# Sums of squares of a residual stage: six chunks added on VectorE and summed on TensorE behind the stage's last product

## The chip, the cores and the metric

The kernel runs on one core of one Trainium2 chip. The metric is device time in microseconds (us) of one execution. TensorE does the matrix products, VectorE and ScalarE the work on their inputs and results, GpSimd only a few transfers, and SyncE's queue loads the weights.

## The reference, cut to what matters

Two transformer blocks are computed for 256 tokens of 1024 values, in float32. Five times a branch is added to the residual x, and each time an RMS norm follows, whose divisor is a sum of squares over the 1024 values of a token:

```python
def rms_norm(x, gain):
    xf = x.astype(jnp.float32)
    y = xf * lax.rsqrt(jnp.mean(xf * xf, axis=-1, keepdims=True) + RMS_EPS)
    return (y * gain.astype(jnp.float32)).astype(x.dtype)
...
        x = x + gate_m * (merged @ w_out[l])          # "x1"
        h = rms_norm(x, norm_ffn[l]) * (1.0 + scale_f) + shift_f
        u = causal_dwconv(h @ w_up[l], ffn_conv_w[l], ffn_conv_b[l])
        u_gate, u_val = jnp.split(u, 2, axis=-1)
        x = x + gate_f * ((jax.nn.silu(u_gate) * u_val) @ w_down[l])      # "x2"
...
        x = x + g1_l * y_l                            # "x3" (attention), "x5" (Fourier mix)
        h2_l = (rms_norm_2(x, norm2_g[i]) * (1.0 + sc2_l) + sh2_l).reshape(B * L, D)
...
        x = x + g2_l * f[:B * L].reshape(B, L, D)     # "x4" (feed-forward of the second block)
```

The last feed-forward is a mixture of eight experts. It takes the second half of the time, and nothing of the change lies in it.

## The kernel before

**How x lies.** X is kept transposed: 1024 values of a token lie over 8 chunks of 128 partitions, 256 tokens along the free axis. A sum over a token's values is therefore a sum over the partitions and over the chunks; TensorE makes it with a 128x128 matrix of ones (`one`) as stationary operand, all chunks accumulated in one PSUM bank ("stat").

**Products.** A weight slab (up to 2048 columns, 1 MB) comes in by SyncE's queue, ScalarE rounds it to `whi` (`act_hi`, L1267), VectorE makes the rest `wlo` (`dve_lo`, L1846), and TensorE does three products per weight tile (`three`, L632 to L634). There are NP = 3 pairs of `whi` and `wlo`: ScalarE rounds slab g + 3 once TensorE is done with slab g. `gemm` makes one output of 2 chunks (256 outputs) for all tokens.

**A residual stage.** Each of x1 to x5 ends with four such outputs, c = 0 to 3. For each of them VectorE adds the gated result to two chunks of X (`dve_residual`, L2123), ScalarE squares them into one of three buffers `sqb` (`act_residual`, L1280; 128x512), and TensorE sums the squares (`pe_stats`, L720 and L723: one product of 256 tokens for each half of the buffer). The squares of chunks 2c - 2 and 2c - 1 are summed behind output c; so the sums of chunks 0 and 1, and of 2 and 3, lie between products, that of chunks 4 and 5 directly behind the last product. (In x3 outputs 0 and 1 are made together, and both inner sums lie between outputs 2 and 3.) The last output has its two halves in two banks, so that chunk 6 can be added, squared and summed while chunk 7 is still in work; `pe_stats(.., 6, True)` sums these. Then ScalarE makes the inverse root (`act_stat`, L1294 and L1297), VectorE and ScalarE make the next stage's input (L1912, L1309, L1919), and TensorE goes on. It is kept in work in between by `spare` (L668), products whose results nobody reads, in a fixed number.

**Modulation.** The gates, scales and shifts come from vectors made on VectorE (`dve_mslabs`, L1870 and L1873, into `macc`) that TensorE sums (`pe_mods`, L709). A list says after which product each is due. x1, x3 and x4 have four of them between the last product and the sum of chunks 6 and 7; x2 has some behind its first outputs and none at its end; x5 has none.

**Order.** Each engine runs its instructions in the order written out by hand in `pe_*`, `act_*` and `dve_*`; semaphores tie them. On VectorE the c = 3 residual of x1, x3 and x5 follows the `dve_lo` of c = 2; that of x2 and x4 follows the `dve_lo` of the slab before the last.

Of the kernel before, what the change touches and what calls it, by code (L numbers as in the profile page):

```python
# [15 lines left out]
S = 256  # L16
# [183 lines left out]
def build(nc, a, out):  # L200
# [5 lines left out]
    with ctx:  # L206
# [506 lines left out]
        def pe_stats(ring, name, c, halves=False):  # L713
# [9 lines left out]
            pe.matmul(o, one[:, :], sq[:, S:512], start=False, stop=(c == 6)).then_inc(sq_read.mark(name, c), 1)  # L723
            N.note(("sq_free", name, c), sq_read.now())

        Z_G, Z_S, Z_T = (0, 1, 2), (3, 4), (5, 6, 7)

        def pe_start():
# [145 lines left out]
        def pe_branches():  # L874
            for c in range(4):
                us = [take(BR_G, "br", c, g) for g in range(4 if c == 3 else 3)]
                for s_ in range(2):
                    h, l, nk = yield from slab(st, ("br", c))
                    for part in range(2):
                        g = (0, 1, 1, 2)[2 * s_ + part]  # L880
                        apart = g == 2 and c == 3
                        for m in range(2):
                            o = us[2 + m].t[:, 0:S] if apart else us[g].t[:, m * S:(m + 1) * S]
                            for k in range(4 * part, 4 * part + 4):
                                kk = 8 * s_ + k
                                if c == 0 and m == 0:
                                    pe.wait_ge(*(yield from xlo_done.of("o", kk)))
                                first, last = ((0, 3), (4, 11), (12, 15))[g]
                                cols = slice(m * 128, (m + 1) * 128)
                                t = three(o, (h[:, k, cols], l[:, k, cols]), (OH[:, kk, :], OL[:, kk, :]),  # L890
                                          kk == first and (m == 0 or apart), kk == last)
                            if apart and m == 0:
                                t.then_inc(us[2].fill(), 1)
                        if part == 0:
                            t.then_inc(us[g].fill(), 1)
                    t.then_inc(st.slab_done.mark(st.pg - 1), 1)
                    yield from pe_mods(BR_T, 29 + 2 * c + s_)
                us[-1].told = st.slab_done.now()
            for c in range(4):
                yield from gemm(BR_G, ("out", c), ("out", c), 1, HH, HL, (lambda kk: xlo_done.of("m", kk)) if c == 0 else None, 7, c == 3)  # L900
                if c:
                    yield from pe_stats(BR_L, "x1", 2 * c - 2)
            yield from pe_mods((0, 1, 2, 6), 40.5)
            yield from pe_stats(BR_L, "x1", 6, True)

        F_G, F_T, F_L = (0, 1, 2, 3), (4, 5), (6, 7)

        def pe_ffn():
            for t in range(22):
                if t == 0:  # L910
                    yield from gemm2(F_G, (("up", 0), ("up", 1)), (("ug", 0), ("uv", 0)), HH2, HL2, lambda k: xlo_done.of("h1", k), wait=12)
                elif t > 1:
                    yield from gemm(F_G, ("up", t), (("ug", "uv")[t % 2], t // 2), 1, HH2, HL2, None, 7)
                if t in (2, 3, 6, 7):
                    tb, c4 = (t - 2) // 4, t % 2
                    u = take(F_T, "cT", tb, c4)
                    pe.wait_ge(*(yield from N.of("cn", tb)))
                    for j in range(4):
                        tt = pe.transpose(u.t[:, j * 128:(j + 1) * 128], cn[:, 0, (4 * c4 + j) * 128:(4 * c4 + j + 1) * 128], ident)
                    tt.then_inc(u.fill(), 1)  # L920
                if 10 <= t < 14:
                    yield from pe_stats(F_L, "ctx", 2 * (t - 10))
                yield from pe_mods(F_T, 41 + t)
            for c in range(4):
                yield from gemm(F_G, ("dn", c), ("dn", c), 3, FH, FL, (lambda kk: xlo_done.of("f", kk)) if c == 0 else None, 21, c == 3)
                yield from pe_mods(F_T, 65 + 3 * c)
                if c:
                    yield from pe_stats(F_L, "x2", 2 * c - 2)
            yield from pe_stats(F_L, "x2", 6, True)

        A_G, A_T = (0, 1, 2), (3, 4, 5, 6, 7)
# [44 lines left out]
        def pe_attention():  # L976
# [53 lines left out]
                             {1: lambda: side(20), 3: lambda: side(21), 4: lambda: side(22)})  # L1030
            for c in (2, 3):
                yield from gemm(A_G, ("wo", c), ("wo", c), 1, HHc, HLc, None, 7, c == 3)
                if c == 2:
                    yield from pe_stats(A_T, "x3", 0)
                    yield from pe_stats(A_T, "x3", 2)
            yield from pe_stats(A_T, "x3", 4)
            yield from pe_mods(A_T, 90.5)
            yield from pe_stats(A_T, "x3", 6, True)

        def pe_ff2():  # L1040
            yield from gemm2(F_G, (("f", 0), ("f", 1)), (("f1", 0), ("f3", 0)), HH4, HL4, lambda k: xlo_done.of("h3", k), wait=12)
            for t in range(2, 28):
                yield from gemm(F_G, ("f", t), (("f1", "f3")[t % 2], t // 2), 1, HH4, HL4, None, 7)
                yield from pe_mods(F_T, 91 + t)
            for c in range(4):
                yield from gemm(F_G, ("f2", c), ("f2", c), 4, FH4, FL4, (lambda kk: xlo_done.of("f2", kk)) if c == 0 else None, 27, c == 3)
                if c:
                    yield from pe_stats(F_L, "x4", 2 * c - 2)
            yield from pe_mods((4, 5, 7, 1), 134.5)
            yield from pe_stats(F_L, "x4", 6, True)  # L1050

        X_G, X_L = (0, 1, 2, 3, 4, 5), (6, 7)

        def pe_fourier():
            pe.wait_ge(*(yield from N.of("fcs")))
            for g in range(8):
                u = take(X_G, "fn1", g)
                if g == 0:
                    spare(u.t[:, 0:128], 9)
                pe.wait_ge(*(yield from act_step.of("fx", g)))  # L1060
                for tb in range(2):
                    t = pe.matmul(u.t[:, tb * 256:tb * 256 + 256], FX[:, g, tb * 128:tb * 128 + 128], fcs[:, 0:256], start=True, stop=True)
                t.then_inc(u.fill(), 1)
            for g in range(0, 8, 2):
                u = take(X_G, "fn2", g)
                for m in range(2):
                    pe.wait_ge(*(yield from N.of("FN", g + m)))
                    for s_ in range(4):
                        tb, part = s_ // 2, s_ % 2
                        t = pe.matmul(u.t[:, m * S:(m + 1) * S], FN[:, tb, g + m, part * 128:part * 128 + 128],  # L1070
                                      fcs[:, 256 + tb * 512 + part * 256:512 + tb * 512 + part * 256], start=(s_ == 0), stop=(s_ == 3))
                t.then_inc(u.fill(), 1)
            for c in range(4):
                yield from gemm(X_G, ("fn", c), ("fn", c), 1, HH5, HL5, (lambda kk: N.of("h4", kk)) if c == 0 else None, 7, c == 3)
                if c:
                    yield from pe_stats(X_L, "x5", 2 * c - 2)
            yield from pe_stats(X_L, "x5", 6, True)

        M_G, M_T = (0, 1, 2), (3, 4, 5)
# [1032 lines left out]
        def dve_residual(name, key, c, gate, d, g0):  # L2112
# [4 lines left out]
            for m in range(2):  # L2117
# [8 lines left out]
                else:  # L2126
                    t.then_inc(u.sem, 1)
                    N.note(("xh", name, m) if c == 3 else ("x", name, c), u.drained())

        def dve_branches():  # L2130
            for c in range(4):
                G_ = (GT1, GT2)[c // 2]
# [33 lines left out]
                yield from dve_mslabs(st.gi[31 + 2 * c + NP])  # L2166
            yield from dve_coeff("h1", 8, "norm_ffn", 0, 8)
            for c in range(4):
                yield from dve_residual("x1", "out", c, modT[0][:, 16:24], 0, 4)
                if c < 3:  # L2170
                    yield from dve_lo(st, 37 + c + NP)
# [11 lines left out]
        def dve_ffn():  # L2183
# [28 lines left out]
            for c in range(4):  # L2212
# [9 lines left out]
                if c == 3:  # L2222
                    yield from ctx
                    yield from dve_coeff("h2", 24, "n10", 1, 2)
                yield from dve_residual("x2", "dn", c, modT[0][:, 40:48], 0, 10)
            yield from dve_modulate("h2", X, HH2, HL2, 24, 1, 0, sqb)
            yield from dve_lo(st, 74 + NP)
# [53 lines left out]
        def dve_attention():  # L2281
# [29 lines left out]
            yield from dve_mods(86)  # L2311
            yield from dve_coeff("h3", 32, "n20", 1, 8)
            for c in range(4):
                yield from dve_residual("x3", "wo", c, modT[1][:, 16:24], 1, 4)
                if c < 3:
                    yield from dve_lo(st, 87 + c + NP)
# [5 lines left out]
        def dve_ff2():  # L2322
# [14 lines left out]
            for c in range(4):  # L2337
# [4 lines left out]
                        yield from dve_mslabs(st.gi[g + NP + 1])  # L2342
                if c == 3:
                    yield from dve_coeff("h4", 40, "n11", 3, 2)
                yield from dve_residual("x4", "f2", c, modT[1][:, 40:48], 1, 10)

        def dve_norm_full(name, dst, col):
# [9 lines left out]
        def dve_fourier():  # L2357
# [18 lines left out]
            dve.wait_ge(*(yield from dve_step.of("xb", 7)))  # L2376
            yield from dve_coeff("h5", 48, "n21", 3, 8)
            for c in range(4):
                yield from dve_residual("x5", "fn", c, modT[3][:, 16:24], 3, 4)
                if c < 3:  # L2380
                    yield from dve_lo(st, g + NP)
                g += 1
# [352 lines left out]
```

## Time and profile before

| | us |
|---|---|
| median of 3 runs | 2139.26 |
| lowest, highest | 2139.07, 2550.09 |
| the profiled execution | 2141.42 |
| its span | 2140.1 |

### The profile page before, as it was taken

What the parts mean: (1) busy time and instruction counts of PE and PEld (TensorE: products, weight loads), DVE (VectorE), ACT (ScalarE), POOL (GpSimd) and SP (SyncE); (2) the same over time, 40 slices, a digit from 0 to 9 for tenths busy, and PEclk for the clock granted to TensorE, in tenths of its full rate; (3) what the DMA queues carried; (4) which work ended last, traced back from release to release, by engine and by line L of the source; (5) the groups of instructions that cost most, each with busy time, mean ns of one, the idle gap of its engine ahead of it and who ended that gap; (6) DMA issues with size and microseconds to landing.
All of it is one profiled execution on the core that took longest, in us unless ns stands there. A gap on an engine that the chain in (4) does not pass through costs nothing.

```text
span 2140.1 us, 30800 instructions
## 1 busy us (share of the span) xinstructions
PE 2071.0 (97%) x12749; PEld 1844.1 (86%) x12749; DVE 1709.2 (80%) x1846; ACT 1260.1 (59%) x1270; POOL 39.4 (2%) x77
## 2 busy tenths in 40 slices
PE   4999999899999999999999999999999999999997
PEld 4887899899898999999997888888888888888886
DVE  6777787799768776777547989898888988888886
ACT  3457643545443454344346777777777777777775
POOL 3000000000000000000000000000000000000000
PEclk8999999989999999999999999999999999999999
DMA  9853476467764346888727999999999999999993
GB/s 311 269 172 113 148 249 198 157 212 245 237 197 165 135 158 199 292 293 269 228 69 274 366 359 357 356 360 363 356 362 350 362 360 358 358 359 361 361 372 146
DMA packets 332802, 580.73 MB, mean 271 GB/s; under 512 B 10357, under 2 KB 150155, under 8 KB 332656
## 3 DMA queue, kind: packets, MB, share of 16 engines
q1 hardware_dynamic: 329152, 572.57, 76.7%
q0 software_dynamic: 3008, 5.78, 1.2%
q8 instruction: 104, 1.70, 0.3%
q10 hardware_dynamic: 496, 0.33, 0.1%
q14 instruction: 42, 0.34, 0.0%
HBM read 577.56 MB, written 1.07 MB: 270 GB/s over the span
## 4 chain that ended last, share of the span: by engine, by line
PE 84%; DVE 9%; ACT 3%; issue 2%; DMA 0%; SPq 0%; DVEq 0%; ACTq 0%
PE bk L638 14%; PE bk L640 14%; PE bk L639 14%; PE bk L632 9%; PE bk L634 9%; PE bk L633 9%; DVE macc L1873 3%; DVE wlo L1846 2%; PE bk L709 1%; ACT whi L1267 1%; PE bk L1159 1%; PE bk L694 1%; DVE uc L2192 1%; PE bk L695 1%; PE bk L696 1%
## 5 line engine op out<-in xcount | busy, mean ns | idle before, releaser
L1846 DVE TENSOR_TENSOR wlo<-raw,whi 128x2048 fp32r<-128x2048 f32 x475 | 1080.6, 2277 | 264.7 <-ACT whi L1267 263.9
L1267 ACT CAST whi<-raw 128x2048 fp32r<-128x2048 f32 x475 | 902.5, 1901 | 390.2 <-PE bk L640 258.8
L632 PE MATMUL bk<-HH,whi 128*128 128x256 f32 x1480 | 430.4, 291 | 6.7 <-DVE HL L1919 6.1
L633 PE MATMUL bk<-HL,whi 128*128 128x256 f32 x1480 | 421.0, 284 | 0.0
L634 PE MATMUL bk<-HH,wlo 128*128 128x256 f32 x1480 | 420.8, 284 | 0.0
L638 PE MATMUL bk<-whi,xh 128*128 128x512 f32 x896 | 354.6, 396 | 0.0
L640 PE MATMUL bk<-wlo,xh 128*128 128x512 f32 x896 | 349.5, 390 | 0.0
L639 PE MATMUL bk<-whi,xl 128*128 128x512 f32 x896 | 348.8, 389 | 0.0
L632 PEld LDWEIGHTS bk<-HH,whi 128*128 128x128 f32 x1480 | 286.7, 194 | 11.3 <-issue 8.5
L633 PEld LDWEIGHTS bk<-HL,whi 128*128 128x128 f32 x1480 | 286.8, 194 | 1.7 <-issue 1.0
L634 PEld LDWEIGHTS bk<-HH,wlo 128*128 128x128 f32 x1480 | 286.3, 193 | 0.0
L1873 DVE SCALAR_TENSOR_TENSOR macc<-raw,csil,macc 128x512 f32<-128x512 f32 x280 | 209.9, 751 | 9.3 <-DMA raw<-in_w_mod 0.5
L640 PEld LDWEIGHTS bk<-wlo,xh 128*128 128x128 f32 x896 | 168.1, 188 | 36.0
L638 PEld LDWEIGHTS bk<-whi,xh 128*128 128x128 f32 x896 | 168.3, 188 | 34.3 <-DVE wlo L1846 1.4
L639 PEld LDWEIGHTS bk<-whi,xl 128*128 128x128 f32 x896 | 168.5, 188 | 33.3
L638 PE MATMUL bk<-whi,tth 128*128 128x512 f32 x448 | 177.5, 396 | 1.7 <-DVE ttl L2490 1.7
L640 PE MATMUL bk<-wlo,tth 128*128 128x512 f32 x448 | 177.7, 397 | 0.0
L639 PE MATMUL bk<-whi,ttl 128*128 128x512 f32 x448 | 177.5, 396 | 0.0
L632 PE MATMUL bk<-FH,whi 128*128 128x256 f32 x400 | 114.6, 286 | 0.0
L633 PE MATMUL bk<-FL,whi 128*128 128x256 f32 x400 | 113.3, 283 | 0.0
L634 PE MATMUL bk<-FH,wlo 128*128 128x256 f32 x400 | 113.2, 283 | 0.0
L638 PEld LDWEIGHTS bk<-whi,tth 128*128 128x128 f32 x448 | 84.3, 188 | 22.1 <-DVE ttl L2490 1.9
(369 smaller groups left out, 2583.0 us busy)
## 6 DMA issues: line engine op xcount, KB each, us to landing
raw<-in_moe_w SPq DMA_DIRECT2D x336, 1024.0 KB, 6.1
raw<-in_ada_w SPq DMA_DIRECT2D x48, 1024.0 KB, 5.3
raw<-in_ff_w SPq DMA_DIRECT2D x40, 1024.0 KB, 5.3
raw<-in_w_in SPq DMA_DIRECT2D x29, 1024.0 KB, 5.4
raw<-in_w_mod SPq DMA_DIRECT2D x24, 1024.0 KB, 5.6
raw<-in_w_up SPq DMA_DIRECT2D x22, 1024.0 KB, 5.1
raw<-in_attn_w_qkv SPq DMA_DIRECT2D x12, 1024.0 KB, 5.1
raw<-in_w_branch SPq DMA_DIRECT2D x8, 1024.0 KB, 5.3
```

Source lines behind the costliest of these rows:

```text
L632: pe.matmul(o, sh, mh, start=start, stop=False, skip_group_check=True)
L633: pe.matmul(o, sh, ml, start=False, stop=False, skip_group_check=True)
L634: return pe.matmul(o, sl, mh, start=False, stop=stop, skip_group_check=True)
L638: pe.matmul(o, sh, mh, start=start, stop=False, skip_group_check=True)
L639: pe.matmul(o, sl, mh, start=False, stop=False, skip_group_check=True)
L640: return pe.matmul(o, sh, ml, start=False, stop=stop, skip_group_check=True)
L694: pe.matmul(o, xh[:, k, c], h[:, k, :], start=(k == 0), stop=False)
L695: pe.matmul(o, xl[:, k, c], h[:, k, :], start=False, stop=False)
L696: t = pe.matmul(o, xh[:, k, c], l[:, k, :], start=False, stop=(k == 7))
L1267: act.copy(whi[k][:, :n], raw[q.slot[i]][:, :n]).then_inc(q.hi_done.mark(g), 1)
L1846: dve.tensor_tensor(wlo[k][:, :n], raw[q.slot[i]][:, :n], whi[k][:, :n].bitcast(F), ALU.subtract).then_inc(q.taken.mark(i), 1)
L1873: t = dve.scalar_tensor_tensor(out=acc[:, :], in0=v[:, j, :], scalar=sc, in1=acc[:, :], op0=ALU.mult, op1=ALU.add)
```

## The change

The sums of chunks 0 to 5 are no longer made one by one. `dve_squares` adds the three buffers of squares on VectorE, in two additions of 128x512, ahead of the residual of c = 3. `pe_stats_sum` sums the result over the partitions with one pair of products; it stands behind the last product and, where there are four modulation sums (x1, x3, x4), behind these. The sum of chunks 6 and 7 follows as before. The two `pe_stats` between the products are gone in all five stages.

```diff
+        def pe_stats_sum(ring, name):
+
+            u = take(ring, "stat", name)
+            pe.wait_ge(*(yield from dve_step.of("squares", name)))
+            sq = sqb[N.at["sq", name, 4]]
+            pe.matmul(u.t[:, 0:S], one[:, :], sq[:, 0:S], start=True, stop=False)
+            pe.matmul(u.t[:, 0:S], one[:, :], sq[:, S:512], start=False, stop=False).then_inc(sq_read.mark(name, 4), 1)
+            N.note(("sq_free", name, 4), sq_read.now())
...
             for c in range(4):
                 yield from gemm(BR_G, ("out", c), ("out", c), 1, HH, HL, (lambda kk: xlo_done.of("m", kk)) if c == 0 else None, 7, c == 3)
-                if c:
-                    yield from pe_stats(BR_L, "x1", 2 * c - 2)
             yield from pe_mods((0, 1, 2, 6), 40.5)
+            yield from pe_stats_sum(BR_L, "x1")
             yield from pe_stats(BR_L, "x1", 6, True)
...
                 yield from pe_mods(F_T, 65 + 3 * c)
-                if c:
-                    yield from pe_stats(F_L, "x2", 2 * c - 2)
+            yield from pe_stats_sum(F_L, "x2")
             yield from pe_stats(F_L, "x2", 6, True)
...
                 yield from gemm(A_G, ("wo", c), ("wo", c), 1, HHc, HLc, None, 7, c == 3)
-                if c == 2:
-                    yield from pe_stats(A_T, "x3", 0)
-                    yield from pe_stats(A_T, "x3", 2)
-            yield from pe_stats(A_T, "x3", 4)
             yield from pe_mods(A_T, 90.5)
+            yield from pe_stats_sum(A_T, "x3")
             yield from pe_stats(A_T, "x3", 6, True)
...
+        def dve_squares(name):
+
+            for n in (1, 2):
+                yield from sq_done.of(name, 2 * n)
+                k = [N.at["sq", name, c] for c in (0, 2, 4)[:n + 1]]
+                for c in (2 * n - 2, 2 * n):
+                    dve.wait_ge(*(yield from sq_done.of(name, c)))
+                dve.tensor_tensor(sqb[k[n]][:, :], sqb[k[n]][:, :], sqb[k[n - 1]][:, :], ALU.add).then_inc(
+                    dve_step.mark(*(("squares", name) if n == 2 else ("squares0", name))), 1)
+                dve.wait_ge(*dve_step.now())
+                N.note(("sq_free", name, 2 * n - 2), dve_step.now())
...
             for c in range(4):
+                if c == 3:
+                    yield from dve_squares("x1")
                 yield from dve_residual("x1", "out", c, modT[0][:, 16:24], 0, 4)
```

x4 is changed as x1 is, x5 as x2 (it has no modulation sums), and `dve_squares` stands ahead of the c = 3 residual in all five.

## Rows read from the trace of the kernel before

**Rows 1.** The page's first part: busy time and share by engine

```profile
PE 2071.0 (97%) x12749; PEld 1844.1 (86%) x12749; DVE 1709.2 (80%) x1846; ACT 1260.1 (59%) x1270; POOL 39.4 (2%) x77
```

**Rows 2.** Waits of TensorE, whole span: us in total, times, longest

```profile
PE bk L709 <- DVE macc L1873: 22.8, 7, 5.1
...
PE bk L638 <- DVE ttl L2490: 1.7, 1, 1.7
```

**Rows 3.** Timeline of TensorE in x1: start us, us, instruction, count

```profile
361.91 0.28 PE L634 MATMUL bk<-HH,wlo 128*128 128x256 f32 x1
362.04 0.60 PE L720 MATMUL bk<-sqb,one 128*128 128x256 f32 x2
...
362.71 0.47 PE L632 MATMUL bk<-HH,whi 128*128 128x256 f32 x1
363.02 0.28 PE L633 MATMUL bk<-HL,whi 128*128 128x256 f32 x1
```

**Rows 4.** VectorE: the same form of addition, and two dependent instructions

```profile
L2144 DVE TENSOR_TENSOR GT<-GT x4: 691/692/694, 316.0 to 349.7; 128x512 f32<-128x512 f32 x4
...
170.40 0.69 DVE L2028 TENSOR_TENSOR rt<-O 128x512 f32<-128x512 f32 x1
171.12 0.43 DVE L2030 TENSOR_SCALAR rt<-rt 128x512 f32<-128x512 f32 x1
```

**Rows 5.** Timelines of the ends of x1 and x4, TensorE

```profile
375.27 0.60 PE L720 MATMUL bk<-sqb,one 128*128 128x256 f32 x2
...
376.14 4.55 PE L709 MATMUL bk<-one,macc 128*128 128x1 f32 x32
...
1066.88 3.63 PE L709 MATMUL bk<-one,macc 128*128 128x1 f32 x32
```

**Rows 6.** Timeline of the end of x5, VectorE and TensorE

```profile
1115.48 2.29 DVE L1846 TENSOR_TENSOR wlo<-raw,whi 128x2048 fp32r<-128x2048 f32 x1 [1.06 <-ACT whi L1267]
1117.69 0.48 DVE L2123 SCALAR_TENSOR_TENSOR X<-bk,mod_a,X 128x256 f32<-128x256 f32 x1
...
1119.81 0.59 PE L720 MATMUL bk<-sqb,one 128*128 128x256 f32 x2
...
1121.10 0.59 PE L723 MATMUL bk<-sqb,one 128*128 128x256 f32 x2
```

**Rows 7.** Timeline of TensorE between outputs 2 and 3 of x2

```profile
599.41 1.02 PE L709 MATMUL bk<-one,macc 128*128 128x1 f32 x8 [1.64 <-DVE macc L1873]
600.30 1.03 PE L720 MATMUL bk<-sqb,one 128*128 128x256 f32 x2
...
601.62 0.77 PE L632 MATMUL bk<-FH,whi 128*128 128x256 f32 x1
```

**Rows 8.** Timeline of the end of x2: ScalarE, VectorE, TensorE

```profile
614.54 1.90 ACT L1267 CAST whi<-raw 128x2048 fp32r<-128x2048 f32 x1 [3.86 <-PE bk L634]
...
616.47 2.29 DVE L1846 TENSOR_TENSOR wlo<-raw,whi 128x2048 fp32r<-128x2048 f32 x1 [3.47 <-ACT whi L1267]
...
618.76 0.87 DVE L2123 SCALAR_TENSOR_TENSOR X<-bk,mod_m,X 128x256 f32<-128x256 f32 x2
...
618.66 0.60 PE L720 MATMUL bk<-sqb,one 128*128 128x256 f32 x2
...
619.74 0.70 PE L720 MATMUL bk<-sqb,one 128*128 128x256 f32 x2
...
620.52 0.47 PE L632 MATMUL bk<-HHc,whi 128*128 128x256 f32 x1
```

**Rows 9.** Stretches in x1 and x2; granted clock is third from the end

```profile
379.00:385.00 6.00, 6.00 (x25) 5.64 (x26) 1.41 (x5) 1.64 (x4) 0.00 (x0) 0.50 0.01 4
571.90:573.00 1.10, 0.01 (x1) 0.00 (x0) 1.10 (x1) 0.00 (x0) 0.00 (x0) 1.00 0.00 0
573.50:577.00 3.50, 0.07 (x1) 0.10 (x1) 3.39 (x6) 0.00 (x0) 0.00 (x0) 0.50 0.60 163
600.50:603.50 3.00, 3.00 (x12) 2.63 (x12) 3.00 (x4) 0.00 (x0) 0.00 (x0) 0.50 1.03 340
```

More of the change, by code:

```diff
@@ L1046, in pe_ff2 @@
                 yield from gemm(F_G, ("f2", c), ("f2", c), 4, FH4, FL4, (lambda kk: xlo_done.of("f2", kk)) if c == 0 else None, 27, c == 3)
-                if c:
-                    yield from pe_stats(F_L, "x4", 2 * c - 2)
             yield from pe_mods((4, 5, 7, 1), 134.5)
+            yield from pe_stats_sum(F_L, "x4")
             yield from pe_stats(F_L, "x4", 6, True)
@@ L1074, in pe_fourier @@
                 yield from gemm(X_G, ("fn", c), ("fn", c), 1, HH5, HL5, (lambda kk: N.of("h4", kk)) if c == 0 else None, 7, c == 3)
-                if c:
-                    yield from pe_stats(X_L, "x5", 2 * c - 2)
+            yield from pe_stats_sum(X_L, "x5")
             yield from pe_stats(X_L, "x5", 6, True)
@@ L2224, in dve_ffn @@
                     yield from dve_coeff("h2", 24, "n10", 1, 2)
+                if c == 3:
+                    yield from dve_squares("x2")
                 yield from dve_residual("x2", "dn", c, modT[0][:, 40:48], 0, 10)
@@ L2313, in dve_attention @@
             for c in range(4):
+                if c == 3:
+                    yield from dve_squares("x3")
                 yield from dve_residual("x3", "wo", c, modT[1][:, 16:24], 1, 4)
@@ L2344, in dve_ff2 @@
                     yield from dve_coeff("h4", 40, "n11", 3, 2)
+                if c == 3:
+                    yield from dve_squares("x4")
                 yield from dve_residual("x4", "f2", c, modT[1][:, 40:48], 1, 10)
@@ L2378, in dve_fourier @@
             for c in range(4):
+                if c == 3:
+                    yield from dve_squares("x5")
                 yield from dve_residual("x5", "fn", c, modT[3][:, 16:24], 3, 4)
```

## Prediction

> **What bounds the kernel now.** I read the page's busy times first: TensorE is busy for 97% of the span, VectorE for 80% [rows 1]. So what counts is whether TensorE has fewer product times to run or fewer waits. The table of TensorE's waits comes next: its largest entry is 22.8 us in seven waits for `macc`, none longer than 5.1, and the largest in the experts is 1.7 us [rows 2]. The second half is therefore a stream of products that only moves as a whole: what is gained or lost ahead of it arrives at the end. Last I read the timelines around the five residual stages, since the gain depends on who is late there.
>
> **What is taken out of the product stream.** In x1 the last product of output 1 starts at 361.91, the second product of output 2 at 363.02: 1.11 us with a pair of sums between them [rows 3]. Products start 0.12 to 0.13 us apart (361.91 and 362.04), so without the pair it would be 0.24. One pair costs 1.11 - 0.24 = 0.87 us. Two such pairs lie between products in each stage, ten in all. In x1, x3, x4 and x5 they run at full clock, so each of these stages has 2 x 0.87 = 1.74 us less product time. The pair directly behind the last product is not saved: the change replaces it by the pair on the sum. In the stages with modulation sums it only changes places with them.
>
> **What VectorE gets.** Two additions of 128x512 float32 from SBUF. The same form takes 692 ns, and an instruction that needs the result of such a one starts 0.72 us after it [rows 4]. Per stage 2 x 0.72 = 1.44 us. The bounds are narrow (2 x 0.69 = 1.38 from below, 2 x 0.75 = 1.5 with a little for a semaphore), and I take 1.44. Their inputs, ScalarE's squares of c = 2, have long been there. They stand ahead of the residual of c = 3, and this residual, its squares on ScalarE, the sum and the root queue behind them. No transfer is issued or moved; SyncE's queue sees only slabs that come free earlier by the gain, and GpSimd's queue sees nothing.
>
> **x1, x3, x4: hidden.** Behind the last product TensorE has four modulation sums. They take 4.55 us in x1 and 3.63 in x4 (x3 is like x4) [rows 5]. VectorE's 1.44 us of additions and the residual behind them fit below this, so the sum is ready before TensorE asks for it. Without this cover it would cost as in x2. I take the whole 1.74 us each, 5.22 together. From below: the data of the next stage must be ready when the spare products end. The pair now stands behind the modulation sums, so the root starts 0.87 us later counted from the last product. I estimate a loss of 0 to 0.3 us a stage for it and take 0.
>
> **x5: nearly hidden.** No modulation sums here. `dve_lo` starts at 1115.48 and VectorE is free 2.21 us later [rows 6]. It waits for ScalarE's rounding, which waits for output 2, and only one of the two pairs lies ahead of that. So it moves by 0.87: VectorE is free at 1116.82, the sum of squares ready at 1118.26. TensorE's last product ends for the sums' start at 1119.81 - 1.74 = 1118.07. It waits some 0.25 us with the semaphore. The residual's halves follow at 1118.26 and 1118.7, their squares end by 1119.6, just when the pair on the sum and the first half of the last pair are done. The last product starts near 1119.65 and not at 1121.10 [rows 6]. Gain 1.46 us.
>
> **x2: a loss.** First, of the two pairs one brings nothing. TensorE idles 1.64 us for `macc` behind output 2 [rows 7], and VectorE's chain up to this point (residual, squares, rounding, `dve_lo`, `macc`) runs without waiting for TensorE. When TensorE comes 0.87 us earlier it waits 0.87 us longer. The other pair runs at half clock from 600.30 to 601.62. What follows would be at half clock instead, so I count its full-clock price, 0.87 to 0.9 us. So the last product of x2 comes 0.9 us earlier, at 617.76 for 618.66 [rows 8]. VectorE's `dve_lo` starts at 616.47, released by ScalarE's rounding at 614.54, which TensorE released inside output 3 [rows 8]: it moves by 0.9 too. Before, the residual started at 618.76 and TensorE waited until 619.74 for the squares, having filled the time with a pair. Now the additions come first: 618.76 - 0.9 + 1.44 = 619.3. TensorE is through with its last product at about 618.0 and waits 1.3 us. The pair takes 0.87 to 620.2. Meanwhile VectorE and ScalarE have done the residual and the square of chunk 6. The last pair follows to about 621.05, where the next product started at 620.52 before [rows 8]. Loss 0.53 us.
>
> **The sum.** 3 x 1.74 + 1.46 - 0.53 = 6.15 us. The profiled execution took 2141.42 us with a span of 2140.1; its median is 2139.26, 2.16 lower (0.1%). Span after: 2134.0, profiled execution 2135.3, median 2139.26 - 6.15 = **2133.1 us**. That is 0.3% and far within 2%, which is about what a measurement of this kernel can tell from no change; a pair of medians may still show the sign.
>
> **The clock, first from rows.** TensorE is at 1.2 GHz from 379 to 385 in x1, where it only did modulation sums before, and from 600.5 to 603.5 in x2, behind an idle of 1.64 us and 0.9 us of modulation sums [rows 9, 7]. In the idle of 5.0 us that starts at 571.9 it still is at 2.4 GHz in the first 1.1 us and at 1.2 from 573.5 [rows 9]. The new wait of 1.3 us at the end of x2 lies near these cases. The Trainium skill says in "TensorE: Matmul & The Clock Gate", section "A second HAM failure mode: psum-queue depth-cycling", that frequent short idles between groups of products are enough to swing the clock. By that rule the change costs more in x2 than the sum has, and the trace agrees in so far as 1.64 us with sparse work behind it sufficed. By the rows alone I take no fall: the work on both sides of the wait is dense, which it was not in the two cases with a fall.
>
> **The rivals.**
> - *The clock falls in x2's new wait.* A stretch at 1.2 GHz is at least 3.0 us long (600.5 to 603.5) [rows 9]; with its edges I take 3.4 as an estimate, and half of it is lost: 1.7 us. Gain 6.15 - 1.7 = 4.4, time 2134.8. For it: the cases above. Against it: dense work to 618.0 and again from 619.3. Chance 0.15.
> - *The clock is better in x1.* There the slow stretch is at least 6.0 us long (379 to 385), two of the others [rows 9]. Its modulation sums now start 1.74 us earlier than before and 0.87 us sooner behind the last product, and a dense pair comes behind them; with one stretch of 3.4 us less, another 1.7 us comes back. Gain 7.85, time 2131.4. For it: modulation sums took 4.55 us in x1 and 3.63 in x4 for the same 32 instructions, so some were slow. Against it: nothing fixes where the stretch starts. Chance 0.2.
> - *The gain is given back.* Seven waits for `macc` [rows 2] and the hand-made order could swallow what arrives early, as in x2. If x1's gain of 1.74 goes in the waits of x1's following stage and x3 and x4 lose 0.3 each at the spare products' end, the gain is 6.15 - 1.74 - 0.6 = 3.8; if half of x3's and x4's goes too, 2.1: time 2135.5 to 2137.2. Against it: those VectorE chains start from TensorE's own results and move along. Chance 0.13.
> - *Slower than before: VectorE is late in every stage.* If the additions were exposed in all five stages, because the residual's squares and not the modulation sums are awaited last, each would cost 1.44 and the pair on the sum 0.87 more: 5 x 2.31 = 11.55 against 10 x 0.87 = 8.7 saved: 2.85 us slower, 2142.1. It decides once VectorE gets to the additions later than about 2 us behind the last product of x1, x3 and x4. In rows 5 the modulation sums take 3.6 us or more, so I hold this for unlikely. Chance 0.03.
> - *No change,* within 1 us of before, because the pairs were idle time in disguise. Rows 3 show products right on either side of a pair, so chance 0.02.
>
> **How the numbers follow.** My forecast (2132.4 to 2134.2, by 0 to 0.3 us in three stages and 0.3 us for the additions and the semaphores) has 0.47. Range 2130.8 to 2136.8: it takes in the forecast, both clock cases and the better half of the given-back gain, and leaves out some 0.12. Every case lies within 2% of 2139.26: faster by over 2% 0.01, same 0.98, slower 0.01.
>
> **What would show it.** Right: L720 and L723 between products gone; products 0.12 us apart over the border of outputs in x1; additions of about 0.69 us on VectorE ahead of the c = 3 residual; the new pair behind L709 in x1, x3, x4 with no idle ahead of it; in x2 an idle of about 1.3 us ahead of the new pair; experts of the same length, starting some 6 us earlier. Wrong: an idle ahead of the pair in x1, x3 or x4; a granted clock of 0.50 right behind x2; the idle for `macc` in x2 no longer than before; a stretch between stages that grew by what a stage gained.

## The result, and the profile after

| | before | after |
|---|---|---|
| median, us | 2142.29 (11 runs) | 2134.45 (11 runs) |
| ratio, 95% interval | 1 | 0.9971 (0.9963 to 0.9978) |
| the profiled execution, us | 2141.42 | 2133.55 |
| its span, us | 2140.1 | 2132.2 |

Two of the eleven runs of before took 2550.09 and 9489.25 us, and the ratio leaves them out. It makes the kernel 6.2 us faster (4.7 to 7.9, as 0.0029, 0.0022 and 0.0037 of 2142.29); the two medians as they stand differ by 7.8, and by 7.0 without the two runs (2141.43). The forecast was 6.15 us. Its 2133.1 us stood on a median of three runs, 2139.26, which was 3.0 us too low as the start; the time of after lies 1.35 us above the forecast.

The first part of the page of the kernel after, to be read beside [rows 1]:

```profile
PE 2055.7 (96%) x12709; PEld 1829.3 (86%) x12709; DVE 1715.9 (80%) x1856; ACT 1259.1 (59%) x1270; POOL 39.4 (2%) x77
```

TensorE has 40 instructions less: 60 of the old sums gone (15 pairs of products, two instructions for each product) and 20 of the new ones added (five pairs). VectorE has ten more. TensorE's waits and two of its groups in the kernel after, beside [rows 2] (us in total, times, longest; then count, busy us and mean ns of one):

```profile
PE bk L709 <- DVE macc L1875: 24.6, 7, 5.2
...
PE bk L731 <- DVE sqb L2139: 1.7, 2, 1.5
```

```profile
L720 PE MATMUL bk<-sqb,one 128*128 128x256 f32 x26 | 9.1, 436 | 0.0
...
L731 PE MATMUL bk<-sqb,one 128*128 128x256 f32 x10 | 4.4, 532 | 1.7 <-DVE sqb L2139 1.7
```

The waits for `macc` grew by 1.8 us in all, and TensorE waits for the new sum in two of five stages only: 1.5 us in x2 and 0.15 in x5. Now the places themselves. x1 in the kernel after: the border between outputs 1 and 2 on TensorE, against [rows 3], and the stage's end on VectorE and TensorE, against [rows 5]:

```profile
362.39 0.28 PE L633 MATMUL bk<-HL,whi 128*128 128x256 f32 x1
362.51 0.28 PE L634 MATMUL bk<-HH,wlo 128*128 128x256 f32 x1
362.63 0.28 PE L632 MATMUL bk<-HH,whi 128*128 128x256 f32 x1
...
372.74 1.41 DVE L2139 TENSOR_TENSOR sqb<-sqb,sqb 128x512 f32<-128x512 f32 x2
...
374.16 4.14 PE L709 MATMUL bk<-one,macc 128*128 128x1 f32 x32
...
378.16 1.20 PE L731 MATMUL bk<-sqb,one 128*128 128x256 f32 x2
```

Products are 0.12 us apart where the pair stood. The two additions take 1.41 us and end at 374.15, where the modulation sums only begin; TensorE asks for the sum 4.0 us later. x2 in the kernel after, behind output 2 and at the end, against [rows 7] and [rows 8]:

```profile
598.33 1.27 PE L709 MATMUL bk<-one,macc 128*128 128x1 f32 x8 [2.81 <-DVE macc L1875]
...
614.46 2.29 DVE L1848 TENSOR_TENSOR wlo<-raw,whi 128x2048 fp32r<-128x2048 f32 x1 [3.47 <-ACT whi L1269]
...
616.75 1.41 DVE L2139 TENSOR_TENSOR sqb<-sqb,sqb 128x512 f32<-128x512 f32 x2
618.20 0.88 DVE L2125 SCALAR_TENSOR_TENSOR X<-bk,mod_m,X 128x256 f32<-128x256 f32 x2
618.31 0.67 PE L731 MATMUL bk<-sqb,one 128*128 128x256 f32 x2 [1.50 <-DVE sqb L2139]
...
619.96 0.47 PE L632 MATMUL bk<-HHc,whi 128*128 128x256 f32 x1
```

The idle for `macc` grew from 1.64 to 2.81 us: the pair ahead of it brought nothing. At the end the additions stand between `dve_lo` and the residual, and TensorE waits for them. x4 and x5 in the kernel after, against [rows 5] and [rows 6]:

```profile
1061.25 3.63 PE L709 MATMUL bk<-one,macc 128*128 128x1 f32 x32
...
1062.87 1.41 DVE L2139 TENSOR_TENSOR sqb<-sqb,sqb 128x512 f32<-128x512 f32 x2
...
1064.74 0.68 PE L731 MATMUL bk<-sqb,one 128*128 128x256 f32 x2
```

```profile
1110.89 1.41 DVE L2139 TENSOR_TENSOR sqb<-sqb,sqb 128x512 f32<-128x512 f32 x2
...
1112.45 0.67 PE L731 MATMUL bk<-sqb,one 128*128 128x256 f32 x2 [0.15 <-DVE sqb L2139]
1112.96 0.59 PE L732 MATMUL bk<-sqb,one 128*128 128x256 f32 x2
1113.39 0.64 PE L720 MATMUL bk<-sqb,one 128*128 128x256 f32 x2
1113.87 0.59 PE L723 MATMUL bk<-sqb,one 128*128 128x256 f32 x2
```

In x4 the additions end at 1064.28, under the modulation sums; TensorE asks for the sum at 1064.74: hidden with 0.46 us to spare by the start of that product.

**The account, stretch by stretch.** Each number is the distance in us between the starts of two instructions in one trace. "End of x2" is from TensorE's last product of x2 to the first product of the next stage; "inside" covers the outputs before it. A second trace of each kernel and a third of after stand beside the first ones.

| stretch | before | before again | after | after again | after, third |
|---|---|---|---|---|---|
| inside x1 (from the c = 1 residual) | 12.91 | 12.91 | 11.20 | 11.19 | 11.20 |
| end of x1 | 11.31 | 11.31 | 11.33 | 9.99 | 11.34 |
| on to x2's first `macc` wait | 190.47 | 191.99 | 190.48 | 193.20 | 190.45 |
| from the first to the second `macc` wait | 22.48 | 22.47 | 22.48 | 22.48 | 22.48 |
| from the second `macc` wait to x2's last product | 19.13 | 20.63 | 18.20 | 19.71 | 18.19 |
| end of x2 | 1.98 | 1.98 | 3.43 | 3.44 | 3.44 |
| on to the first residual of x3 | 179.89 | 179.90 | 178.74 | 179.89 | 178.71 |
| inside x3 | 13.54 | 13.54 | 11.82 | 11.82 | 11.83 |
| end of x3 | 9.67 | 9.64 | 9.98 | 9.99 | 9.99 |
| on to the c = 1 residual of x4 | 208.24 | 208.62 | 208.32 | 208.32 | 208.31 |
| inside x4 (from the c = 1 residual) | 34.04 | 34.04 | 32.31 | 32.31 | 32.31 |
| end of x4 | 9.04 | 7.78 | 7.79 | 7.79 | 7.79 |
| inside x5 | 24.21 | 24.21 | 22.47 | 22.47 | 22.47 |
| end of x5, to its last pair of sums | 1.41 | 1.41 | 1.85 | 1.85 | 1.85 |

Two kinds of rows stand out. Those inside x1, x3, x4 and x5 agree to 0.01 us within a kernel and step by what the change does. Those "on to" a later place, the way to x2's last product, and the ends of x1 and x4 can differ between traces of the same kernel, by 0.4 to 2.8 us: in the longer ones TensorE mostly shows half the clock for some 3 us more. In the pair first profiled this favoured after by 1.15 us ahead of x3 (before ran at 0.54 from 665.7 to 669.0, after at 1.00 there) and by 1.25 in x4.

### The profile page after: what moved, and what is told of

Same layout as the page of the kernel before. It is cut to its first block, busy times and chain, and to the rows that moved or that the text cites. A ratio compares the mean times of both kernels' runs of the same rounds, so it can differ in the third digit from the quotient of the medians.

```text
span 2132.2 us, 30745 instructions
## 1 busy us (share of the span) xinstructions
PE 2055.7 (96%) x12709; PEld 1829.3 (86%) x12709; DVE 1715.9 (80%) x1856; ACT 1259.1 (59%) x1270; POOL 39.4 (2%) x77
## 3 DMA queue, kind: packets, MB, share of 16 engines
q8 instruction: 103, 1.69, 0.3%
## 4 chain that ended last, share of the span: by engine, by line
PE 83%; DVE 10%; ACT 3%; issue 3%; DMA 1%; SPq 0%; DVEq 0%; ACTq 0%
PE bk L638 14%; PE bk L640 14%; PE bk L639 14%; PE bk L632 9%; PE bk L634 9%; PE bk L633 9%; DVE macc L1875 3%; DVE wlo L1848 2%; ACT whi L1269 1%; PE bk L709 1%; PE bk L1161 1%; DVE uc L2208 1%; PE bk L694 1%; PE bk L696 1%; PE bk L695 1%
```

## The experiments

**The pairs put back.** The changed kernel, and two pairs of products per stage where the old sums stood, with nothing read from them.

```diff
+        def pe_pair(ring, name, c):
+            if c == 0:
+                take(ring, "stat", name)
+            for _ in range(2):
+                pe.matmul(B.at["stat", name].t[:, 0:S], one[:, :], cst[:, 0:S], start=True, stop=True)
...
+                if c in (1, 2):
+                    pe_pair(BR_L, "x1", 2 * c - 2)
```

> The changed kernel with the two pairs of products per stage put back between the outputs, on constants instead of the squares; their result is not used. What is left of the change is VectorE's additions and the pair on the sum. Theory A: product time is that of the kernel before; x1, x3, x4 cost nothing, x5 nothing (VectorE is ready 0.7 us before the last product), x2 1.4 us. Time 1.4 us over the kernel before (ratio 1.0007). Rival B (the gain is mainly the clock's, from the work behind the modulation sums): most of the gain of 6 us stays, 3 us or more below the kernel before.

2143.37 us (median of 10), ratio to before 1.0005 (0.9996 to 1.0015): the gain is gone, and the middle of the interval lies 1.1 us on the slow side, where the additions' cost should put it. Its stretches inside x1, x3 and x4 are 12.91, 13.54 and 34.04, those of before, and x5 has 24.31 for 24.21; the end of x2 stays 3.44, that of after. The pairs are what the change gains, and they cost product time.

**x2 left as it was,** the other four stages changed.

```diff
-            yield from pe_stats_sum(F_L, "x2")
+                if c:
+                    yield from pe_stats(F_L, "x2", 2 * c - 2)
...
-                if c == 3:
-                    yield from dve_squares("x2")
```

> The changed kernel with stage x2 alone put back as it was. Theory A: from the end of the macc wait behind output 1 of x2 to the first product of the attention stage it takes 0.5 us less than in the changed kernel (43.6 us as before, against 44.1), the wait for macc behind output 2 is 1.64 us again and not 2.81, and the time is 0.5 us below the changed kernel. If the changed x2 gained as the other stages do, this would be 1.7 us over it.

2138.22 us in one run, 3.8 over the changed kernel's median where 0.5 below it was expected; one run says nothing at this size, and 2.95 us of it lie in the end of x4, which took 10.74 us for 7.79 though this kernel has x4 as after has it. The stretches of x2 say more: 20.60 from the second `macc` wait to x2's last product and 1.98 at the end, as in "before again" (20.63, 1.98; both with the long stretch at half clock). "After again", with the same clock, has 19.71 and 3.44. So 22.58 us against 23.15: the change loses 0.57 us in x2. With the short stretch, before and after of the first profiles have 21.11 and 21.63, a loss of 0.52. TensorE's second wait for `macc` in the experiment, where the old pair behind output 1 is back:

```profile
598.42 1.83 PE L709 MATMUL bk<-one,macc 128*128 128x1 f32 x8 [2.21 <-DVE macc L1876]
```

It is 2.21 us, in before again 2.17, in after again 3.11. The 0.90 to 0.94 us between them are the swallowed pair.

**Twice the vector work.** Each addition gets a maximum of the same size ahead of it, of a buffer with itself, which leaves the values as they are.

```diff
+                dve.tensor_tensor(sqb[k[n]][:, :], sqb[k[n]][:, :], sqb[k[n]][:, :], ALU.max).then_inc(
+                    dve_step.mark("again", name, n), 1)
+                dve.wait_ge(*dve_step.now())
```

> The changed kernel with the additions' VectorE time doubled: ahead of each of the ten additions the buffer is replaced by the maximum of itself and itself, which leaves its values as they are. Theory A: each stage gets 1.4 us more on VectorE ahead of the last residual. x2 pays all of it (its wait ahead of the new pair grows from 1.50 to 2.9 us), x5 pays it too (0.15 to 1.6 us), x4 about 1.0 us (additions ended at 1064.28, TensorE came for the sum at 1064.74), x1 and x3 nothing (4 us of modulation sums lie over it). Sum 3.8 us over the changed kernel. Rival C (the additions cost in every stage): 7 us over it. Rival B: no relation to the additions, only the clock moves.

2143.68 us. TensorE's waits for the sum in x2, x4 and x5, all there are:

```profile
620.54 1.19 PE L731 MATMUL bk<-sqb,one 128*128 128x256 f32 x2 [2.95 <-DVE sqb L2142]
...
1072.03 1.19 PE L731 MATMUL bk<-sqb,one 128*128 128x256 f32 x2 [1.00 <-DVE sqb L2142]
...
1123.52 0.67 PE L731 MATMUL bk<-sqb,one 128*128 128x256 f32 x2 [1.60 <-DVE sqb L2142]
```

Against after they grew by 1.45, 1.00 and 1.45 us. In x2 and x5 the work is exposed in full, in x4 all but the 0.4 us of slack, in x1 and x3 not at all. But the end of x2 took 6.43 us where 3.43 + 1.45 = 4.9 was due, and the end of x4 11.35 where 7.79 + 1.00 = 8.8 was: another 1.5 and 2.6 us, with TensorE at half clock. In x4 the wait isn't the cause: it begins at 1071.03, and the clock, third from the end in this view of stretches, fell just ahead of it:

```profile
1069.50:1070.90 1.40, 1.40 (x14) 1.40 (x13) 1.33 (x3) 0.00 (x0) 0.00 (x0) 1.00 0.46 64
1070.95:1077.70 6.75, 5.75 (x19) 4.98 (x19) 2.90 (x11) 1.97 (x5) 0.00 (x0) 0.50 0.38 144
```

The total is one run, 9.2 us over the changed kernel's median and so above both theories' sums (3.8 and 7). It can't decide between them. The waits can: they are those of the first theory.

**The sum ahead of the modulation sums** in x1, x3 and x4: the cover is taken away.

```diff
+            yield from pe_stats_sum(BR_L, "x1")
             yield from pe_mods((0, 1, 2, 6), 40.5)
-            yield from pe_stats_sum(BR_L, "x1")
```

> The changed kernel with the pair on the sum ahead of the four modulation sums in x1, x3 and x4, so that nothing covers the additions there. My prediction said that without this cover it would cost as in x2. By the trace of the changed kernel the additions end 0.1 us around the last product in x1 (374.15 against 374.16) and x3 (810.65 against 810.64), and 3.0 us behind it in x4 (1064.28 against 1061.25). So by theory A as the trace now reads: a wait of 0 to 0.2 us in x1 and x3, of 3.0 us in x4, some 3 us over the changed kernel. As the prediction was written: 1.4 us in each of the three, 4.2 us.

2143.12 us in one run, 8.7 over the changed kernel's median for the 3 or 4.2 expected; what it gave beyond its waits stands below. TensorE in x1 and in x4 (the rest of the wait table has only x2's 1.50 and x5's 0.15 for the sum):

```profile
374.59 0.28 PE L634 MATMUL bk<-HH,wlo 128*128 128x256 f32 x1
374.85 0.67 PE L731 MATMUL bk<-sqb,one 128*128 128x256 f32 x2
```

```profile
1066.45 0.67 PE L731 MATMUL bk<-sqb,one 128*128 128x256 f32 x2 [3.02 <-DVE sqb L2139]
```

In x1 and x3 the profile has no wait even without the cover; the pair starts 0.26 us behind the last product there, where products are 0.12 apart. The additions follow the `dve_lo` of c = 2, which ends 1.2 us ahead of the start of the last product in x1 (373.37 and 374.59), and are over about when TensorE comes. Only in x4, whose additions stand behind a `dve_lo` that starts near the end of the stage as in x2, is the cover needed. The end of x4 took 15.60 us, not 7.79 + 3.02 = 10.8. (The ends of x1 and x3 took 8.52 and 11.53 for 11.33 and 9.98, the first at full clock throughout, the second at a mean granted clock of 0.70 for 0.82.) In this view TensorE's busy time stands behind the length:

```profile
1063.50:1066.40 2.90, 0.00 (x0) 0.00 (x0) 2.83 (x5) 0.00 (x0) 0.00 (x0) 1.00 0.19 38
1067.60:1077.10 9.50, 9.50 (x42) 9.13 (x41) 0.65 (x4) 0.76 (x3) 0.00 (x0) 0.50 0.19 72
```

Behind a wait of 3.0 us TensorE ran for 9.5 us at 1.2 GHz.

**The two long waits again, open and filled.** The first kernel has both: the doubled work in x2 alone, and the sum ahead of the modulation sums in x4 alone. The second is the same with eleven spare products (results unread) run in each wait.

```diff
+            yield from pe_stats_sum(F_L, "x4")
             yield from pe_mods((4, 5, 7, 1), 134.5)
-            yield from pe_stats_sum(F_L, "x4")
...
+                if name == "x2":
+                    dve.tensor_tensor(sqb[k[n]][:, :], sqb[k[n]][:, :], sqb[k[n]][:, :], ALU.max).then_inc(
+                        dve_step.mark("again", name, n), 1)
+                    dve.wait_ge(*dve_step.now())
```

```diff
             u = take(ring, "stat", name)
+            if name in ("x2", "x4"):
+                spare(u.t[:, 0:128], 11)
             pe.wait_ge(*(yield from dve_step.of("squares", name)))
```

> In x2 each addition is preceded by a maximum of the same size (values unchanged), and in x4 the pair on the sum stands ahead of the modulation sums. Both waits of TensorE for the sum should then be about 3 us long (2.95 and 3.02 in the two earlier runs that did this). Theory A, a wait costs its own length only: from x2's last product to the next stage's first 3.43 + 1.45 = 4.9 us, and from x4's last product to the Fourier stage's first 7.8 + 3.0 = 10.8 us. Theory D, a wait of 3 us also brings TensorE's clock down for what follows, as in the two earlier runs: 6.4 us in x2 and about 15.6 us in x4.

> As e8_two_waits, but TensorE runs eleven spare products (22 instructions, at full clock some 2.65 us) in each of the two waits, so that it is idle for 0.3 to 0.4 us only. The length of the wait is the same. Theory D (the idle time brings the clock down): granted clock 1.00 behind x2's end, 4.9 us there instead of 6.4; in x4 at most 10.8 to 12.2 us instead of 15.6, the modulation sums at full clock or as before the change. Theory A (the wait costs its own length, and the rest in the earlier runs was chance): no difference between this run and e8_two_waits in either place. If the clock falls because of the sparse modulation sums alone, x4 stays near 13 to 15.6 us here and x2 alone is better.

2148.41 us open, 2142.02 filled. The view of stretches, open kernel: the wait in x2, what follows, the wait in x4, what follows:

```profile
617.00:619.90 2.90, 0.00 (x0) 0.00 (x0) 2.76 (x6) 0.00 (x0) 2.34 (x5) 0.96 0.56 178
620.00:623.00 3.00, 3.00 (x7) 2.44 (x8) 0.72 (x2) 0.81 (x2) 0.74 (x2) 0.50 1.25 305
1067.10:1070.00 2.90, 0.00 (x0) 0.00 (x0) 2.83 (x5) 0.00 (x0) 0.00 (x0) 1.00 0.27 50
1070.50:1078.00 7.50, 7.50 (x34) 7.23 (x33) 0.82 (x4) 0.79 (x2) 0.00 (x0) 0.50 0.34 129
```

The same places in the filled kernel; the last line is the stretch behind the modulation sums of x4:

```profile
617.40:620.00 2.60, 2.57 (x23) 2.38 (x22) 2.50 (x6) 0.00 (x0) 1.92 (x4) 1.00 0.52 134
620.40:623.00 2.60, 2.60 (x14) 2.16 (x15) 0.83 (x2) 1.28 (x3) 0.85 (x2) 1.00 1.22 357
...
1068.00:1072.00 4.00, 4.00 (x33) 3.90 (x34) 1.18 (x5) 0.81 (x2) 0.00 (x0) 0.99 0.70 253
1072.70:1078.00 5.30, 5.30 (x22) 4.94 (x23) 2.40 (x7) 2.54 (x7) 0.00 (x0) 0.50 0.01 2
```

The end of x2 took 6.39 us open and 4.89 filled, the end of x4 17.25 and 13.71. In x2 this is the whole difference between the two theories: a wait of 2.95 us costs its length, and 1.5 us of clock on top unless TensorE is kept at work. In x4 it is not so clean. 13.71 is more than the 10.8 to 12.2 expected and lies where the expectation put "the sparse modulation sums alone". The filled wait leaves the clock up for the sum's pair and most of the modulation sums, then it falls after all, and 13.71 is 2.9 us over the 10.8 of the wait alone. That is what a fall costs there with no wait at all (10.74 for 7.79 in the kernel with x2 as it was). And each kernel has one trace: against the 15.60 us of the kernel with the sum first the filling won 1.9 us in x4, against the 17.25 of the open one 3.5.

**The additions earlier.** In x1, x3 and x5 the first addition goes behind the residual of c = 2; in x2 and x4 both go ahead of the `dve_lo` at whose end VectorE used to find them.

```diff
+                    if (c, n) == (3, 0):
+                        yield from dve_squares("x2")
...
-                if c == 3:
-                    yield from dve_squares("x2")
```

> The changed kernel with its additions made earlier on VectorE: in x2 and x4 both stand ahead of the first rounding rest of output 3, where VectorE idled 5.8 us (x2) and 1.6 us or more (x4); in x1, x3 and x5 the first addition stands behind the residual of output 2, in an idle of 0.4 to 1.1 us, and only the second one ahead of the last residual. Theory A (the gain is product time taken out, and the additions cost only where they stand on the way to the last residual): x2 loses its wait of 1.50 us ahead of the new pair and ends 1.4 us earlier against its last macc wait, x5 gains up to 0.15 us, x1, x3 and x4 nothing; together 1.5 us below the changed kernel, about 7.7 us below the kernel before (ratio 0.9964). Rival B (the gain is mainly the clock's: fewer stretches at 1.2 GHz): the wait goes but the time stays that of the changed kernel within 0.5 us. Rival C (VectorE's total work is what counts): no change, since the same work is done.

2134.44 us (median of 11), ratio 0.9972 (0.9963 to 0.9981), where the changed kernel has 0.9971 and 0.9964 was expected. It was run again beside the changed kernel:

> The changed kernel once more, unchanged, to stand beside e11_early_2 on the same chip. By both theories 0.9971 of the kernel before (0.9963 to 0.9979); in x2 a wait of 1.50 us ahead of the pair on the sum, 3.43 us from its last product to the next stage's first.

> The kernel with the early additions once more, beside e10_after_3. Theory A: the wait in x2 (1.45 us) and the 0.44 us of x5 are won at no other cost, so 1.9 us less than e10_after_3: 0.9962 of the kernel before where e10_after_3 has 0.9971. Theory B, what is won there is lost elsewhere (VectorE's later work, the clock of TensorE): the same ratio as e10_after_3 within 0.0003.

2135.31 us (7 runs), ratio 0.9974 (0.9963 to 0.9985), for the changed kernel; 2134.56 us (8 runs), ratio 0.9967 (0.9955 to 0.9980), for the early additions. The places came out as meant: no wait for the sum anywhere, the end of x2 1.98 us in both traces and that of x5 1.41, which is 1.46 and 0.44 less than in after. The times don't settle whether 1.9 us is left of it at the end: the ratio fell by 0.0007 in the second comparison and not at all in the first, theory A has 0.0009, and each interval is 0.0009 or more to either side. The traces show what stands against it: the end of x4 took 9.37 and 10.74 us here, and 7.79 in all three traces of after; ahead of x3's first residual it took 179.86 us in both, as in the slower traces of the table. The stretch view of x4's end with the early additions and in the third trace of after:

```profile
1060.00:1074.00 14.00, 14.00 (x81) 13.02 (x80) 7.29 (x19) 5.29 (x13) 0.00 (x0) 0.76 0.36 123
```

```profile
1060.00:1072.00 12.00, 11.80 (x86) 11.10 (x86) 8.66 (x21) 5.89 (x14) 0.00 (x0) 1.00 0.46 158
```

Whether the early additions cause this half clock in x4 or meet it by chance was not separated: it is also there in before (9.04 once, 7.78 once), with the pairs put back (9.36) and with x2 left as it was (10.74).

**The two kernels once more,** for the spread in the table above.

> The kernel before, once more, for its trace: how much the single stages and the stretches at 1.2 GHz differ between two executions of one kernel. I expect the product stream between waits to agree within 0.1 us and the stretches at 1.2 GHz to differ in place, which moves a stage by up to 1.7 us either way (attention moved by 1.2 us between the two traces at hand).

> The changed kernel, once more, for its trace. Theory A: the wait ahead of the new pair in x2 is 1.50 us again and in x5 0.15, x2 takes 0.5 us longer than in the kernel before. The attention stage may be 1.2 us longer than in the first trace, since what it gained there was the clock's and not the change's.

2143.53 and 2138.56 us. The first stands 2.1 us above the first profiled execution of its kernel, the second 5.0 above that of after. Of these 5.0, the table has 2.72 - 1.34 around x1, 1.51 in x2 and 1.15 ahead of x3: 4.0 us by the clock. One of them, 2.7 us, is more than the 1.7 expected of a stage.

## Why the prediction was right, step by step

- **Price of a pair, 0.87 us.** It held. Inside x1, x3, x4 and x5, two pairs made 1.71, 1.72, 1.73 and 1.74 us, and putting pairs back gave the old distances again.
- **Additions, 1.44 us.** 1.41 for the two, 1.45 with the semaphore where they are exposed.
- **x1 and x4, hidden.** Yes. x1 gained 1.69 with its end. x4 gained 1.73 inside, the modulation sums cover the additions with some 0.4 us to spare, and at full clock (before again, after) the end took 7.78 before and 7.79 after. The prediction also had the root 0.87 us later behind the last product. It isn't: the pair that now stands behind the modulation sums stood ahead of them before, and L723 starts 4.98 us behind x4's last product before and 4.99 after. In x1 and x3 a reason that I gave was not the one that matters: I counted the modulation sums as cover, but the additions are through before these begin, as the experiment with the sum first shows. "Without this cover it would cost as in x2" is true of x4 alone.
- **x3, the whole 1.74.** 1.72 inside, but in the profiled executions the end grew from 9.67 to 9.98, net 1.40. The estimate had allowed a loss of this size (0 to 0.3 us), for the later root, and then taken 0. In after the four products on sums of squares lie in a stretch at half clock (their starts are 0.99, 0.85 and 0.86 us apart, where x4 at full clock has 0.51, 0.43 and 0.44), and the next stage's `HL` is ready at 820.45, just when the product starts at 820.50; before, only the last of them and the spare products were slow, and TensorE started at 823.62 on data ready at 822.66. The loss goes with the place of the half clock and not with the change: the kernel with the two open waits has x3 as after has it, began its products on sums at full clock and slowed only behind the second (they start at 819.96, 820.47, 820.90 and 821.61), and its end took 9.67 as before. In two others with the same x3 it took 9.78 (x2 as it was) and 11.33 (filled waits). More vector work is not the reason either: with the doubled additions it took 9.66.
- **x5, 1.46.** Measured 1.30. By the prediction TensorE would be ready for the sum at 1118.07 and start it 0.25 us later. x5 starts 5.93 us earlier in after, so this is 1112.14, and the sum starts at 1112.45, 0.31 later (the profile counts 0.15 of it as idle). The pair of chunk 6 then follows the pair on the sum by 0.94 us (1112.45 to 1113.39) instead of 0.87.
- **x2, a loss of 0.53.** 0.52 in the first pair of traces, 0.57 at the other clock. Both halves of the argument were seen apart: the wait for `macc` longer by 1.17 us (0.94 between the two second traces) for the 0.87 expected, with 22.47 or 22.48 us between the two waits in every trace of the table, so VectorE's chain there did not depend on when TensorE came; the wait at the end 1.50 for the 1.3 expected.
- **The clock as a rival.** In x2's new wait it did not fall, in any of three traces of after. The rival's mechanism is real, though, and its price was well sized: at 2.95 us the wait brings a stretch at half clock that costs 1.5 us (1.7 estimated). The rule of the Trainium skill that I weighed ("TensorE: Matmul & The Clock Gate", section "A second HAM failure mode: psum-queue depth-cycling": frequent short idles swing the clock) would have put the loss in x2 already. The traces do not bear it out for the single short waits of 1.50 and 1.41 us, where the clock stayed at 1.00; the falls came with single waits of 2.95 and 3.02 us, twice as long, and no run here tried frequent ones.
- **Better clock in x1.** Not in the first trace of after (11.31 before, 11.33 after). It came in one of three traces of after (9.99), and in the kernel with the filled waits, whose x1 is that of after (8.30, full clock throughout). Both times the stretch behind took 2.7 us more (193.2), so that little or nothing was left.
- **The sum.** By stretches that the change touches, x1 1.69, x2 -0.52, x3 1.40, x4 1.73, x5 1.30: 5.6 us for the 6.15 predicted, or 5.9 with x3's end as with the open waits. The two profiled executions differ by 7.9, because 2.4 us of better clock came on top (1.15 ahead of x3, 1.25 in x4), with 0.6 us lost before x1 and 0.7 gained in the experts, where traces of one kernel differ by more (1017.2 to 1018.5 us from x5's last sum to the end in the three of after). The times can only say that 5.6, 5.9 and 6.15 all lie in the interval of 4.7 to 7.9; that the 6.2 of the ratio comes so near to 6.15 is luck. The terms that the prediction names for its forecast reach down to 2132.8 (2133.1 less 0.3), not to the 2132.4 that it gives.

## What to carry over

Count a removed product as gain only if no wait for another engine comes between it and the end: of ten pairs taken out nine paid, and the tenth only made a wait for `macc` longer. Work moved to another engine is free where that engine reaches it before the consumer does, so look at what stands directly ahead of it in that engine's order: the same 1.4 us cost nothing in x1, x3 and x4, 0.4 in x5 and all of it in x2. When two traces are compared for an effect of 1 us, compare distances between neighbouring instructions, since the clock alone moved two traces of one kernel apart by 4 us, and find a second trace of the same stage before a difference at its end is put down to a change.

## What the runs showed of the hardware

- An idle of TensorE of 1.41 or 1.50 us between dense products left the granted clock at 1.00 behind it (five traces: three of after, one with the sum first, one with the pairs put back), and so did one of 1.60 us in x5 with the doubled work. One of 2.95 to 3.02 us was followed by 0.50 in all four cases, for 3 us in x2 with dense work behind it and for over 7 in x4 with the modulation sums (one column each) behind it. Among modulation sums 0.50 also comes with a shorter idle or none: behind the 1.64 us of idle in x2 before [rows 7, 9], and in x4 with no wait at all (before, and the kernel with x2 as it was).
- The price of that fall can exceed the wait: in x4, 3.0 us of wait brought 4.8 and 6.4 us more (15.60 and 17.25 against 10.8), of which up to 2.95 can come there without a wait (10.74 against 7.79). Spare products in the wait took back 1.5 us in x2 and, by which trace one compares with, 1.9 or 3.5 in x4, though they do nothing for the wait itself.
- Stretches at half clock appear in different places in traces of one kernel. In x2 they made two values: the way from x2's second `macc` wait to its last product was 18.2 or 19.7 us in after and 19.1 or 20.6 in before, never between.
